# Front of an RWKV mixer on one core: narrow first products from own buffers, three products begun on the first tokens, second products between those of a wide unit

## The reference

```python
xx = jnp.pad(h, ((0, 0), (1, 0), (0, 0)))[:, :-1] - h
xs = h[None] + xx[None] * mu[:, None, None, :]
rkv = jnp.einsum('nbtd,nde->nbte', xs[:3], w_rkv)
r, k, v = rkv[0], rkv[1], rkv[2]
xv, xw, xa, xg = xs[2], xs[3], xs[4], xs[5]
w_log = -jax.nn.softplus(-(w0 + jnp.einsum('btl,ld->btd', jnp.tanh(xw @ w1), w2)).astype(jnp.float32)) - 0.5
v = v + (v_first - v) * jax.nn.sigmoid(v0 + (xv @ v1) @ v2)
a = jax.nn.sigmoid(a0 + (xa @ a1) @ a2)
g = jax.nn.sigmoid(xg @ g1) @ g2
```

## Time and profile before

| | us |
|---|---|
| three runs | 1644.9, 1640.95, 1644.88; median 1644.88 |
| span of the profiled execution | 1638.5 |
| front on TensorE, first to last matmul | 710.5 to 941.1 |
| TensorE busy | 1567.2 (96% of the span) |
| VectorE busy | 852.3 (52%) |
| ScalarE busy | 637.0 (39%) |

### The profile page before, as it was taken

How to read it: one execution, slowest core, us unless ns; L and a number is a source line. 1 busy time by engine, 2 the same in 40 slices (tenths; PEclk the granted TensorE clock), 3 DMA queues, 4 the chain that set the end, 5 groups by cost and what they waited for, 6 DMA issues and landing times. The chain is left out here.

```text
span 1638.5 us, 35327 instructions
## 1 busy us (share of the span) xinstructions
PE 1567.2 (96%) x15881; PEld 1410.4 (86%) x15881; DVE 852.3 (52%) x1201; ACT 637.0 (39%) x880; POOL 156.7 (10%) x180
## 2 busy tenths in 40 slices
PE   6999998999999999999999989999789999999997
PEld 5998987999999999989988978888558888888886
DVE  5675665544433444677566545545485444344432
ACT  3654654332212223455566333333244322122322
POOL 3100100001000015000000411101010010001100
PEclk9999999999999999998999989999999999999999
DMA  4112121333332333662222100000303333233331
GB/s 132 53 59 72 53 72 46 91 91 90 105 89 78 91 90 115 176 183 71 62 72 59 39 19 4 4 4 5 106 28 98 94 91 114 81 90 102 100 94 64
DMA packets 225814, 126.41 MB, mean 77 GB/s; under 512 B 8856, under 2 KB 220976, under 8 KB 225408
## 3 DMA queue, kind: packets, MB, share of 16 engines
q1 hardware_dynamic: 225360, 124.07, 25.6%
q10 hardware_dynamic: 304, 0.08, 0.0%
HBM read 117.71 MB, written 6.42 MB: 76 GB/s over the span
## 5 line engine op out<-in xcount | busy, mean ns | idle before, releaser
L125 ACT ACTIVATE w_hi<-w_raw 128x1024 fp32r<-128x1024 f32 (+1 forms) x200 | 224.3, 1122 | 548.0 <-PE psg L785 305.8
L785 PE MATMUL psg<-x_hi,w_hi 128*128 128x264 f32 (+1 forms) x1080 | 350.2, 324 | 1.8 <-DVE w_lo L129 1.8
L785 PE MATMUL psg<-x_lo,w_hi 128*128 128x264 f32 (+1 forms) x1080 | 350.4, 324 | 0.0
L785 PE MATMUL psg<-x_hi,w_lo 128*128 128x264 f32 (+1 forms) x1080 | 349.6, 324 | 0.0
L129 DVE TENSOR_TENSOR w_lo<-w_raw,w_hi 128x1024 fp32r<-128x1024 f32 (+1 forms) x200 | 261.9, 1310 | 139.8 <-ACT w_hi L125 139.6
L785 PEld LDWEIGHTS psg<-x_hi,w_hi 128*128 128x128 f32 x1080 | 202.8, 188 | 20.1 <-DVE w_lo L129 2.2
L785 PEld LDWEIGHTS psg<-x_lo,w_hi 128*128 128x128 f32 x1080 | 202.8, 188 | 17.4 <-issue 0.2
L785 PEld LDWEIGHTS psg<-x_hi,w_lo 128*128 128x128 f32 x1080 | 203.3, 188 | 16.7
L1248 PE MATMUL psg<-mid_hi,w_hi 128*128 128x264 f32 (+1 forms) x528 | 170.8, 323 | 2.5 <-DVE w_lo L129 2.5
L1248 PE MATMUL psg<-mid_lo,w_hi 128*128 128x264 f32 (+1 forms) x528 | 170.0, 322 | 0.0
L1248 PE MATMUL psg<-mid_hi,w_lo 128*128 128x264 f32 (+1 forms) x528 | 169.4, 321 | 0.0
(11 more groups left out here) (389 smaller groups left out, 3182.7 us busy)
## 6 DMA issues: line engine op xcount, KB each, us to landing
w_raw<-in_w_ffn_in_dram SPq DMA_DIRECT2D x88, 512.0 KB, 3.8
w_raw<-in_w_ffn_out_dram SPq DMA_DIRECT2D x40, 704.0 KB, 4.6
w_raw<-in_w_qkv_dram SPq DMA_DIRECT2D x24, 512.0 KB, 3.8
w_raw<-in_w_rkv_dram SPq DMA_DIRECT2D x24, 512.0 KB, 4.1
w_raw<-in_w_o_attn_dram SPq DMA_DIRECT2D x8, 512.0 KB, 4.1
w_raw<-in_w_o_rwkv_dram SPq DMA_DIRECT2D x8, 512.0 KB, 4.2
v_first<-v_pair SPq DMA_DIRECT2D x8, 264.0 KB, 2.0
res_kept<-res SPq DMA_DIRECT2D x1, 2112.0 KB, 7.8
```

Source lines behind the costliest of these rows:

```text
L125: k.nc.scalar.activation(k.w_hi[j][:, 0:kt, :], k.raw[j][:, 0:kt, :], ACT.Copy).then_inc(k.hi_ready[j].h, 1)
L785: done = k.nc.tensor.matmul(k.psg[:, 2 * j + c, 0:size], w[:, t, :], x, start=t == first and n == 0, stop=t == last and n == 2)
```

## The change

First products V1 and W1 are no units any more. Their weights have small buffers (`small_raw`, `small_hi`, `small_lo`: 32 and 64 columns), are loaded by two DMAs right behind the attention stage, ahead of the first MLP's units, and are split once, at the start of that MLP's last halves. Their products (`small_row`) go to two banks of `psx` on 32 and 64 columns. The front has 30 units.

On the first half of the tokens TensorE now runs V1 and two value units, then the rows of the second half for V1 and the first of them, then the second half of the other. On the second products, `unit_beside` runs three rows (18 matmuls) alone, and the other five between the rows of the next wide unit: 3 matmuls of the unit, 6 of the second product, and so on; 33 matmuls of the unit follow alone.

A value unit is read out of PSUM by ScalarE (`v_copy`), and VectorE's three operations then work on SBUF. The load of unit 2 no longer stands behind the store of the residual `res_kept`, the store goes behind the load of `v_first`, and the table of activation functions for the sigmoid is loaded earlier. Three waits are renamed where semaphores were merged.

The diff, cut to its core (the rest is the renumbering of the hand-written orders, of which two places are shown in it, and the merged semaphores):

```diff
     def sync(self, sp):
+        if not self.tail:
+            self.nxt.small_sync(sp)
...
+            first.small_low(dve)
...
+        first.small_high(act)
...
-V1, V2, W1, W2, G1, A1, A2 = 0, 3, 10, 13, 16, 22, 24
-V_UNITS = (1, 2, 4, 5, 6, 7, 8, 9)
-K_UNITS = (11, 12, 14, 15, 18, 19, 20, 21)
-R_UNITS = (23, 25, 26, 27, 28, 29, 30, 31)
-FRONT_UNITS = 32
+V2, W2, G1, A1, A2 = 2, 11, 14, 20, 22
+V_UNITS = (0, 1, 3, 4, 5, 6, 7, 8)
+K_UNITS = (9, 10, 12, 13, 16, 17, 18, 19)
+R_UNITS = (21, 23, 24, 25, 26, 27, 28, 29)
+FRONT_UNITS = 30
...
+    def small_sync(self, sp):
+
+        for n, src in enumerate(self.small_srcs):
+            sp.dma_start(self.r.small_raw[n][:], src).then_inc(self.small_in.h, 16)
+
+    def small_high(self, act):
+
+        act.wait_ge(self.small_in.h, 2 * 16)
+        for n in range(2):
+            self.k.nc.scalar.activation(self.r.small_hi[n][:], self.r.small_raw[n][:], ACT.Copy).then_inc(self.small_r.h, 1)
+
+    def small_low(self, dve):
+
+        dve.wait_ge(self.small_r.h, 2)
+        for n in range(2):
+            self.k.nc.vector.tensor_tensor(self.r.small_lo[n][:], self.r.small_raw[n][:], self.r.small_hi[n][:].bitcast(F32),
+                                           ALU.subtract).then_inc(self.small_r.h, 1)
...
+    def small_ps(self, rank):
+        return self.k.psx[0:rank, 2:4, 0:HALF]
...
-        if n in (MIX_K, MIX_G, MIX_A, MIX_R):
-            self.wait_done(act, {MIX_K: V_UNITS[-1], MIX_G: W1, MIX_A: G1 + 1, MIX_R: K_UNITS[-1]}[n])
+        if n == MIX_G:
+            act.wait_ge(self.small_d.h, 2)
+        if n in (MIX_K, MIX_A, MIX_R):
+            self.wait_done(act, {MIX_K: V_UNITS[-1], MIX_A: G1 + 1, MIX_R: K_UNITS[-1]}[n])
...
-        sp.wait_ge(self.rs_r.h, 2)
-        sp.dma_start(k.res_kept, k.res[:]).then_inc(self.spilled.h, 16)
         for i in range(2, FRONT_UNITS):
             unit_load(k, sp, self.u0 + i, self.srcs[i], KT)
             if i == 3:
+                sp.wait_ge(self.rs_r.h, 2)
                 sp.dma_start(r.kk_in[:, :, PAD:TP], k.v_first).then_inc(self.vf_in.h, 16)
+                sp.dma_start(k.res_kept, k.res[:]).then_inc(self.spilled.h, 16)
...
-        def hidden(i, rank, index):
-
-            self.wait_done(act, i)
-            nc.scalar.activation(r.hid_hi[0:rank, :].rearrange("p (a b) -> p a b", a=2), halves(k, (self.u0 + i) % 2)[0:rank],
+        def hidden_v():
+
+            act.wait_ge(self.small_d.h, 1)
+            nc.scalar.activation(r.hid_hi[0:LORA['v'][2], :].rearrange("p (a b) -> p a b", a=2), self.small_ps(LORA['v'][2]),
                                  ACT.Copy).then_inc(self.hid_h.h, 1)
+
+        def hidden_a():
+
+            self.wait_done(act, A1)
+            rank = LORA['a'][2]
+            nc.scalar.activation(r.hid_hi[0:rank, :].rearrange("p (a b) -> p a b", a=2),
+                                 halves(k, (self.u0 + A1) % 2)[0:rank], ACT.Copy).then_inc(self.hid_h.h, 1)
+
+        def v_copy(m):
+
+            self.wait_done(act, V_UNITS[m])
+            nc.scalar.activation(real(r.vv, m), halves(k, (self.u0 + V_UNITS[m]) % 2), ACT.Copy)\
+                .then_inc(self.freed(V_UNITS[m]), 1)
...
-            act.wait_ge(self.v_step.h, 2 * m + 1)
+            act.wait_ge(self.v_step.h, 3 * m + 3)
...
-        hidden(V1, LORA['v'][2], 0)
+        nc.scalar.preload_act_table_set("sigmoid_and_others")
+        hidden_v()
+        v_copy(0)
         self.weights_hi(act, 2)
+        parts(8, 9)
+        v_copy(1)
         self.weights_hi(act, 3)
-        parts(8, 11)
+        parts(10, 11)
+        second(0, r.rr, vcol(k, 'v0'))
         self.weights_hi(act, 4)
...
+        highs(16, 19)
+        act.wait_ge(self.small_d.h, 2)
+        nc.scalar.activation(r.hid[:].rearrange("p (a b) -> p a b", a=2), self.small_ps(C), ACT.Tanh).then_inc(self.hid_h.h, 1)
+        v_copy(7)
         self.weights_hi(act, 10)
+        highs(20, 23)
+        act.wait_ge(self.hid_h.h, 2)
+        nc.scalar.activation(r.hid_hi[:], r.hid[:], ACT.Copy).then_inc(self.hid_h.h, 1)
         self.weights_hi(act, 11)
...
-            i = V_UNITS[m]
-            j, out = (self.u0 + i) % 2, real(r.vv, m)
-            self.wait_done(dve, i)
+            first, out = r.kk_in[:, m, PAD:TP], r.vv[:, m, PAD:TP]
+            self.wait_freed(dve, V_UNITS[m] if m else V2)
+            nc.vector.tensor_tensor(first, first, out, ALU.subtract).then_inc(self.v_step.h, 1)
             dve.wait_ge(self.turn_r.h, m + 1)
-            nc.vector.tensor_tensor(out, real(r.kk_in, m), halves(k, j), ALU.subtract).then_inc(self.v_step.h, 1)
-            dve.wait_ge(self.v_step.h, 2 * m + 1)
-            nc.vector.tensor_tensor(out, out, real(r.rr, m), ALU.mult).then_inc(self.v_step.h, 1)
-            dve.wait_ge(self.v_step.h, 2 * m + 2)
-            nc.vector.tensor_tensor(out, out, halves(k, j), ALU.add).then_inc(self.freed(i), 1)
-
-        def hidden_low(i, rank, index):
+            dve.wait_ge(self.v_step.h, 3 * m + 1)
+            nc.vector.tensor_tensor(first, first, r.rr[:, m, PAD:TP], ALU.mult).then_inc(self.v_step.h, 1)
+            dve.wait_ge(self.v_step.h, 3 * m + 2)
+            nc.vector.tensor_tensor(out, out, first, ALU.add).then_inc(self.v_step.h, 1)
...
-        hidden_low(V1, LORA['v'][2], 0)
+        hidden_low(0, LORA['v'][2], self.small_ps(LORA['v'][2]), self.hid_l.h)
         self.weights_lo(dve, 2)
+        mixed(8, 9)
         self.weights_lo(dve, 3)
-        mixed(8, 9, 10, 11)
-        self.weights_lo(dve, 4)
+        mixed(10, 11)
         dve.wait_ge(self.vf_in.h, 16)
         v_evict(0)
+        self.weights_lo(dve, 4)
         v_evict(1)
-        self.weights_lo(dve, 5)
...
-        def second(i, rank, which):
+        def second_begin(i):
 
             u = self.u0 + i
-            j = u % 2
-            pe.wait_ge(k.lo_ready[j].h, u // 2 + 1)
-            pe.sem_inc(k.psum_free[j].h, 1)
-            for m in range(KT):
-                s = KT * which + m
-                if s >= 2:
-                    pe.wait_ge(self.turn_r.h, s - 1)
-                for half in range(2):
-                    cols = slice(half * HALF, half * HALF + HALF)
-                    for a, (w, x) in enumerate(((k.w_hi, r.hid_hi), (k.w_hi, r.hid_lo), (k.w_lo, r.hid_hi))):
-                        done = nc.tensor.matmul(k.psx[:, 2 * (m % 2) + half, 0:HALF], w[j][0:rank, m, :], x[0:rank, cols],
-                                                start=a == 0, stop=a == 2)
-                done.then_inc(self.turn_d.h if m < KT - 1 else k.unit_done[j].h, 1)
+            pe.wait_ge(k.lo_ready[u % 2].h, u // 2 + 1)
+            pe.sem_inc(k.psum_free[u % 2].h, 1)
+
+        def second_row(i, rank, which, m):
+
+            j = (self.u0 + i) % 2
+            s = KT * which + m
+            if s >= 2:
+                pe.wait_ge(self.turn_r.h, s - 1)
+            for half in range(2):
+                cols = slice(half * HALF, half * HALF + HALF)
+                for a, (w, x) in enumerate(((k.w_hi, r.hid_hi), (k.w_hi, r.hid_lo), (k.w_lo, r.hid_hi))):
+                    done = nc.tensor.matmul(k.psx[:, 2 * (m % 2) + half, 0:HALF], w[j][0:rank, m, :], x[0:rank, cols],
+                                            start=a == 0, stop=a == 2)
+            done.then_inc(self.turn_d.h if m < KT - 1 else k.unit_done[j].h, 1)
+
+        def unit_beside(i, first, s, rank, which, lead):
+
+            second_begin(s)
+            for m in range(lead):
+                second_row(s, rank, which, m)
+            begin(i)
+            m = lead
+            for c in range(2):
+                for t in range(KT):
+                    row_products(i, first + t, c)
+                    if m < KT:
+                        second_row(s, rank, which, m)
+                        m += 1
+
+        def small_row(which, rank, n, c):
+
+            t, (hi, lo) = n % KT, self.dest(n)
+            at, size = spans[c]
+            w_hi, w_lo = r.small_hi[which], r.small_lo[which]
+            for a, (w, x) in enumerate(((w_hi, hi), (w_hi, lo), (w_lo, hi))):
+                done = nc.tensor.matmul(k.psx[0:rank, 2 + c, 0:HALF], w[:, t, :], x[:, at:at + size],
+                                        start=t == 0 and a == 0, stop=t == KT - 1 and a == 2)
+            if t == KT - 1 and c == 1:
+                done.then_inc(self.small_d.h, 1)
...
-        begin(V1)
+        pe.wait_ge(self.small_r.h, 4)
         for t in range(KT):
             self.wait_low_half(pe, t, 0)
-            row_products(V1, t, 0)
+            small_row(0, LORA['v'][2], t, 0)
             if t == KT // 2:
                 second_sums()
-        begin(V_UNITS[0])
-        for t in range(KT):
-            row_products(V_UNITS[0], t, 0)
+        for i in V_UNITS[0:2]:
+            begin(i)
+            for t in range(KT):
+                row_products(i, t, 0)
         for t in range(KT):
             self.wait_low_half(pe, t, 1)
-            row_products(V1, t, 1)
+            small_row(0, LORA['v'][2], t, 1)
```

(67 more changed lines are left out.)

128 lines of the change are left out of this document (62 added, 66 removed).

## The result

The change makes the kernel slightly slower. In 20 runs of each the median is **1655.4 us** (1642.0 to 1674.8) after and 1644.9 us (1639.6 to 1653.2) before: a ratio of **1.0051, interval 1.0029 to 1.0072**. Each ratio in this document leaves out the runs that lie more than 1.5% above the fastest of their kernel (here 1668.1 and 1674.8 us, so the two medians stand further apart than the ratio says; later 1683.4 and 3032.3 us of e10 and two runs each of e6 and e7). The predicted time was 1634.6 us, and slower had a chance of 0.08. A later series of the same kernel gave 1.0007 (0.9976 to 1.0038), so the loss is between nothing and 0.7%. What has to be explained is why the expected gain of 10 us did not come.

The account below looks back on a forecast made before the run. TensorE, busy 96% of the span, was taken as the bound, with waits and low clock in the front to remove. -5.1 - 2.8 - 2.7 + 0.3 = -10.3 us, from 1644.9 to 1634.6 us; range 1627.0 to 1643.0.

Parts of the forecast that it names:

- What bounds the kernel: Whole span: TensorE busy 96%; only two of 40 clock slices below 9 tenths, both said to lie in the front.
- Start of the front: Front's start to the second value unit's end: ends at 728.5 instead of 735.5, 7.0 us earlier.
- The wait before row 2: In V2: TensorE idles 2.1 us until ScalarE's first sigmoid, with row 2 starting at 732.5.
- V2 and the unit beside it: V2 with its wide unit: clock stays low through V2, end at 748.8 instead of 753.9, 5.1 us earlier.
- W2 and A2: Second products W2 and A2 with the next wide units: gains of 2.8 and 2.7 us from alternation.
- A short dip: In W2 and A2: a brief low-clock stretch, 3.3 us low and 1.7 us lost, as likely as none.
- The low clock spreads: Rival: low clock begins in the lead and lasts through alternation, W2 17.2 us; 1641.6 us in all, chance 0.20.
- Narrow columns lower the clock: Rival, slower: W1's products on 64 columns and V1's on 32 run at low clock; 1650.9 us, chance 0.08.
- High clock throughout: Rival: alternating wide products hold the high clock even at V2; -16.9 us, 1628.0 us, chance 0.20.
- W1 and the first key unit: Around W1: a wait of 1.0 us replaces one of 1.2 us, so no gain.
- Small work: Two small splits at the last halves' start and 0.4 MB of DMA: cost between 0 and 1 us, taken as 0.3.
- The spread row: Profile row: ten records of products on 16 rows in 2.0 us between wide units, at clock 1.00.

Follow-up runs that it names:

- e10: The changed kernel measured a second time, nothing altered, against the kernel before: ratio 1.0007 (0.9976 to 1.0038).
- e6: The kernel before with only its second products put on 128 zero-padded rows: 1643.6 us, ratio 0.9978.
- e7: The changed kernel with second products on 128 rows and V2's first sigmoids ahead of four of ScalarE's parts: 1625.5 us, ratio 0.9885.
- e1: The changed kernel with all eight rows of V2, W2 and A2 ahead of the wide unit, so no alternation: 1638.7 us, ratio 0.9952.

## Why the prediction was wrong

*What bounds the kernel.* One reading was wrong and carried nothing: of the two slices of low clock in the page of before, only the one from 737 to 778 us is in the front. The other, from 942 us, lies behind its end at 941.1.

*Start of the front.* Right. "7.0 us earlier": V2's first product came at 728.86, where 728.9 was worked out. VectorE's rows held it up nowhere.

*The wait before row 2.* Right, within half a microsecond: row 2 begins at 732.2, where 732.5 was predicted, with 1.6 us of it for the sigmoid.

*V2 and the unit beside it.* Wrong. The failed step is "51 matmuls take 51 x 0.22 = 11.2 ... then perhaps 11 more at 0.22". From the first second product the group should have taken 19.9 us (728.9 to 748.8) and took 24.4. The sum counts matmuls alone and puts a switch at nothing, without a reason; ten more switches at 0.3 us are 3.0. And the low clock held on for 26 wide matmuls behind the alternation, not 11: 15 x 0.1 = 1.5. Together 4.5, the whole difference in this profile. In e10 it held on for 17, and the group took 23.0. W1 so began at 782.6 us, where 778 was predicted.

*W2 and A2.* Wrong, for the same two reasons. "I take 2.8 and 2.7" meant groups of 13.5 and 12.9 us. At high clock they take 14.7 and 14.1: the price of ten switches (2.0) on top of the 12.5 and 11.9 that the prediction gave for high clock throughout. At low clock, which came in one of two and two of two profiles, they take 20.6 and 21.4. "A short dip ... is as likely as none" is what failed there: the dip lasts through the alternation.

The three terms make up what the front did. In the first profile the groups are 4.5, 1.2 and 8.5 us over the forecast, 14.2; with the forecast for the front, -10.6 (the +0.3 lies ahead of it), that is +3.6, and the front took 3.9 us more than before. In the second it is 3.1 + 7.1 + 8.5 - 10.6 = +8.1, for 8.3 measured. How far the front makes the median isn't shown: in the first series the medians stand 10.5 us apart, and the changed kernel's profiled execution (1649.0 us) was faster than its median.

*Rivals.* "The low clock spreads" was the right mechanism with the wrong size. It gave W2 17.2 us; with ten switches at 0.3 it would have been 20.2, and 20.6 and 22.0 were measured. It had a chance of 0.20 and a price of +7 against the forecast; with the switches it would have been +7 and another 9, on the slow side. "Narrow columns lower the clock", the rival that would have been slower, is refuted, so that slower came by another way than the one its chance stood for: W1's products on 64 columns ran at 1.00 (within the stretch 755 to 791, all of it at 1.00), and e1 gains what the start promised. It is few rows that are dear here, not few columns. "High clock throughout" held for W2 in one profile, and even that group was 2 us longer than the rival said.

*W1 and the first key unit.* Right: a wait of 1.1 us for 1.0. *Small work* (+0.3): nothing in the runs sets it apart.

The spread row was the ground for hoping that a short lead would do. It was misread: eight of its ten records are products on 16 rows, 0.22 us apart at 1.00, and the other two are wide ones at its ends. They tell the price too: the same gap of 0.21 us stands ahead of them (916.79 to 917.00), and the wide product behind them lasts 0.39. I had read their clock and not their start times.
